# Norms of keys and queries in two chains instead of one in the mixers of a two-block transformer kernel

## The chip, the cores and the metric

The kernel runs on one core of a Trainium2 chip. The metric is the device time of one execution in microseconds (us), the median over several executions.

## The reference

Two transformer blocks of two layers each are applied to one sequence of 256 tokens with 1024 features. The change touches the second block only. Each of its two layers starts with this mixer (`DEPTH` is 2, `DN_HEADS` 4, the head size 128, `T` is 256 tokens):

```python
def l2norm(t):
    return t * lax.rsqrt(jnp.sum(t * t, -1, keepdims=True) + L2_EPS)

def gated_deltanet(q, k, v, z, b_logit, a_logit, sc_w, a_log, dt_bias, on_g):
    qkv = jax.nn.silu(causal_depthwise_conv(jnp.concatenate([q, k, v], -1), sc_w))
    q, k, v = jnp.split(qkv, 3, axis=-1)
    q, k, v = l2norm(heads(q)), l2norm(heads(k)), heads(v)
    beta = jax.nn.sigmoid(b_logit)
    g = -jnp.exp(a_log) * jax.nn.softplus(a_logit + dt_bias)
    o = chunk_gated_delta_rule(q, k, v, g, beta)
    ...

def hybrid_mixer(x, w_in, ...):
    h = x @ w_in
    c_val, c_gate, q, k, v, z, b_logit, a_logit = jnp.split(h, IN_SPLITS_2, axis=-1)
    y_conv = conformer_conv(c_val, c_gate, dw_w, dw_b, cln_g, cln_b)
    y_dn = gated_deltanet(q, k, v, z, b_logit, a_logit, sc_w, a_log, dt_bias, on_g)
    return jnp.concatenate([y_conv, y_dn], axis=-1) @ w_out
```

`conformer_conv` holds a causal depthwise convolution with a window of 31 tokens over 512 channels. `chunk_gated_delta_rule` builds 64-token triangular systems from the normed keys and queries, solves them, and runs a state through the four chunks. After the mixer come a residual, a layer norm, and a feed-forward part: a dense one in the first layer, eight experts in the second. The norms that the change is about are the two `l2norm` calls: for each head and token a sum of 128 squares, its root and its reciprocal, multiplied back onto keys and queries.

## The kernel before

Every engine has one program, written out by hand in a fixed order, and every wait is a wait on a counter of another engine (`pe_done`, `act_done`, `vec_done`, `slots_used`). So a waiting instruction holds back all that is queued behind it on its engine. `mix_tensor`, `mix_scalar` and `mix_vector` hold the mixer's three programs; they run once for `mixA` (first layer) and once for `mixB` (second layer).

TensorE multiplies the transposed activations `xT` with 12 slots of weights from a ring in SBUF that SyncE's queue fills: `project(n)` for n from 0 to 11. One such projection gives two blocks of 128 features in the bank `6 + n % 2` (n = 4 and 5 are the keys, 6 and 7 the queries, 8 and 9 the values, 10 and 11 the gate `z`). "The eighth projection" is `project(7)` and the ninth is `project(8)`. ScalarE copies each out of its bank (`evac(n)`, L1985); `project(n)` waits for `evac(n - 2)`. VectorE then runs a four-tap convolution over it (`short_conv(n)`, L2109 and L2112), and ScalarE a SiLU (`silu(n)`, L1992). For keys and queries VectorE squares the result (`square(n)`, L2120).

Between these, VectorE works off the 31-tap convolution, in portions put among the other work by hand: `taps(n)` (L2827 and L2831) is n taps of two instructions each.

The norms follow one chain for keys and queries together: sums of squares over features by matmuls with a one-hot column (L1774, four for each of k and q, into bank 5), a root on ScalarE (L2016), a reciprocal on VectorE (L2194), the high half in fp32r on ScalarE (L2019) and the low half on VectorE (L2196), and the broadcast of both halves to 128 partitions by four matmuls for each of the two (`broadcast`, L1718, steps `bck` and `bcq`). VectorE multiplies the keys with their norm (L2203), the keys with beta (L2208, from banks 0 and 1, step `bcb`), and the queries with theirs (L2212). Then come the products of keys with keys and queries (L1786), the masked matrices (L2223 to L2239), the transposes of the keys (L1743), the second half of the last projection, and the triangular solve. `row_both` holds two rows, one broadcast each; `norms` is a tile of 4 partitions with 512 columns, 256 for the keys and 256 for the queries.

The order on the engines in this stretch of the kernel before is:

- TensorE: `project(7)`, `project(8)`, the sums, `project(9)`, `bck` and `bcq`, `project(10)`, the key products.
- ScalarE: `evac(7)`, `silu(7)`, `evac(8)`, root, high half, `silu(8)`, `evac(9)`.
- VectorE: `square(7)`, `taps(8)`, reciprocal, low half, `short_conv(8)`, the three multiplications.

Of the kernel before, what the change touches and what calls it, by code (L numbers as in the profile page):

```python
# [17 lines left out]
F32 = mybir.dt.float32  # L18
# [4 lines left out]
ALU = mybir.AluOpType  # L23
AX = mybir.AxisListType

P = 128
# [114 lines left out]
def build(nc, x_d, stream, par1_d, par2_d, con_d, out, known):  # L141
    ctx = ExitStack()
    with ctx:
# [1549 lines left out]
        def mix_tensor(pe, tag, layer, last):  # L1693
# [14 lines left out]
            def project(n):  # L1708
                w = rg.take(pe).rearrange("p (k n) -> p k n", n=UNIT)
                if n >= 2:  # L1710
                    pe.wait_ge(act_done, AC.at(tag + f"ev{n - 2}"))
                project_half(n, w, 0)
                project_half(n, w, 1).then_inc(slots_used, 1)

            def broadcast(banks, j, name):

                for h in range(4):
                    mm = pe.matmul(PS[banks[h // 2]][:, (h % 2) * T:(h % 2 + 1) * T], sel_both[0:36, h * P:(h + 1) * P],  # L1718
                                   row_both[0:36, j, :], start=True, stop=True)
                mm.then_inc(pe_done, PE.step(tag + name))  # L1720
# [43 lines left out]
            pe.wait_ge(vec_done, VE.at(tag + "gb.lo"))  # L1764
            broadcast((2, 3), 0, "bcg")
            broadcast((0, 1), 1, "bcb")
            for n in range(5, 9):
                project(n)

            pe.wait_ge(vec_done, VE.at(tag + "sq"))  # L1770
            for n, name in enumerate("kq"):
                y = sq[name][:, :, :].rearrange("p t n -> p (t n)").rearrange("p (b t) -> p b t", t=T)
                for h in range(4):
                    mm = pe.matmul(PS[5][0:4, n * T:(n + 1) * T], hot[:, 3 - h:7 - h], y[:, h, :],  # L1774
                                   start=(h == 0), stop=(h == 3))
            mm.then_inc(pe_done, PE.step(tag + "ssq"))
            project(9)
            pe.wait_ge(vec_done, VE.at(tag + "kq.lo"))
            broadcast((4, 5), 0, "bck")
            broadcast((2, 3), 1, "bcq")  # L1780
            project(10)
            pe.wait_ge(vec_done, VE.at(tag + "kq"))
            for t in range(NT):
# [177 lines left out]
        def mix_scalar(act, tag, layer, last):  # L1961
# [20 lines left out]
            def evac(n):  # L1982
                act.wait_ge(slots_used, used(n + 1))
                func = {"cg": ACT.Sigmoid, "z": ACT.Silu}.get(MIX_SLOTS[n][0], ACT.Copy)
                act.activation(evac2(n), PS[6 + n % 2][:, :].rearrange("p (a b) -> p a b", a=2), func)\  # L1985
                   .then_inc(act_done, AC.step(tag + f"ev{n}"))
# [21 lines left out]
            for n in range(4, 8):  # L2008
                evac(n)
                silu(n)  # L2010
                if n == 5:
                    act.wait_ge(vec_done, VE.at(tag + "ex"))
                    act.activation(scr[:, 0, :], scr[:, 0, :], ACT.Exp).then_inc(act_done, AC.step(tag + "ET"))
            evac(8)
            act.wait_ge(pe_done, PE.at(tag + "ssq"))
            act.activation(norms, PS[5][0:4, :], ACT.Sqrt, bias=eps_rms[0:4, 0:1]).then_inc(act_done, AC.step(tag + "l2r"))  # L2016
            act.wait_ge(vec_done, VE.at(tag + "rn"))
            act.wait_ge(pe_done, PE.at(tag + "bcb"))
            act.activation(row_both[0:4, :, :], norms.rearrange("p (j t) -> p j t", j=2), ACT.Copy)\  # L2019
               .then_inc(act_done, AC.step(tag + "kq.hi"))  # L2020
            silu(8)
            evac(9)
            act.wait_ge(pe_done, PE.at(tag + "bcq"))
            act.activation(row_both[0:4, 0, :], rows[4], ACT.Copy).then_inc(act_done, AC.step(tag + "e.hi"))
            silu(9)
# [62 lines left out]
        def mix_vector(v, tag, layer, last):  # L2088
# [36 lines left out]
            def taps(n):  # L2125
                for pair, w in itertools.islice(tap, n):
                    v_taps(v, tag, pair, w, w + 1)
# [45 lines left out]
            for t in range(NT):  # L2173
                for h in range(4):
# [6 lines left out]
            short_conv(5)  # L2181
            taps(3)
            square(5)
            short_conv(6)
            taps(3)
            square(6)
# [1 line left out]
            short_conv(7)  # L2188
            taps(3)
            square(7)  # L2190
            VE.mark(tag + "sq")
            taps(8)
            v.wait_ge(act_done, AC.at(tag + "l2r"))
            v.reciprocal(norms, norms).then_inc(vec_done, VE.step(tag + "rn"))  # L2194
            v.wait_ge(act_done, AC.at(tag + "kq.hi"))
            v.tensor_tensor(row_both[32:36, :, :], norms.rearrange("p (j t) -> p j t", j=2),  # L2196
                            row_both[0:4, :, :].bitcast(F32), ALU.subtract).then_inc(vec_done, VE.step(tag + "kq.lo"))
            short_conv(8)

            v.wait_ge(pe_done, PE.at(tag + "bck"))  # L2200
            for i in range(2):
                half = slice(i * 512, (i + 1) * 512)
                v.tensor_tensor(dkf[:, half], dkf[:, half], PS[4 + i][:, :], ALU.mult).then_inc(vec_done, VE.step())  # L2203
            v_wait(v)
            v.wait_ge(pe_done, PE.at(tag + "bcb"))
            for i in range(2):
# [2 lines left out]
            v.wait_ge(pe_done, PE.at(tag + "bcq"))  # L2209
            for i in range(2):  # L2210
                half = slice(i * 512, (i + 1) * 512)
                v.scalar_tensor_tensor(out=dqf[:, half], in0=dqf[:, half], scalar=float(P) ** -0.5, in1=PS[2 + i][:, :],  # L2212
                                       op0=ALU.mult, op1=ALU.mult).then_inc(vec_done, VE.step())
            VE.mark(tag + "kq")
            short_conv(9)
# [813 lines left out]
```

## Time and profile before

| what | value |
|---|---|
| median of three runs | 2625.47 us (2623.07 to 2625.53) |
| span of the profiled execution, first to last instruction | 2620.8 us |
| median less that span | 4.7 us |
| TensorE busy | 97% of the span |
| VectorE busy | 73% |
| ScalarE busy | 53% |
| mean granted TensorE clock | 0.981 |

No time of its own is listed for the profiled execution, only its span; the three timed runs lie 2.3 to 4.8 us above it. The first mixer's stretch lies around 990 to 1184 us of the span and the second's around 1380 to 1556 us. The profile's busy times are added over the whole program; the rows below are from the stretch that the change touches. A time in a row of the chain of waits is the time that the instruction added to the chain; a time in the timeline is the instruction's duration, and overlaps its neighbour by some 0.08 us on VectorE.

### The profile page before, as it was taken

The numbers are of one execution on the slowest core, as the hardware profiler recorded it, in microseconds if no ns is written. First come the engines' busy times: TensorE is split into PE (matmuls) and PEld (weight loads), VectorE is DVE, ScalarE is ACT, GpSimd is POOL, SyncE is SP. The second block draws the span as 40 slices with busy tenths as digits, with TensorE's granted clock in tenths as the row PEclk, the third lists the DMA queues.
The fourth block names the chain that finished last, engine by engine and source line by source line (L and its number), as shares of the span: only waits on it lengthen the run. The fifth ranks groups of instructions, "written<-read, shape, count | busy, mean of one in ns | idle before, by whom it ended". The sixth has DMA issues, their size and how long they took to land.

```text
span 2620.8 us, 36271 instructions
## 1 busy us (share of the span) xinstructions
PE 2532.1 (97%) x14798; PEld 2195.6 (84%) x14798; DVE 1914.5 (73%) x2221; ACT 1399.9 (53%) x1490; POOL 0.2 (0%) x4
## 2 busy tenths in 40 slices
PE   7999999999999999999999999999999999999897
PEld 7999889899898998869988767888888888888786
DVE  7765755577675546956447958898989898988797
ACT  4554544456454433224333226777777777777674
POOL 0000000000000000000000000000000000000000
PEclk9999999999999999999999998999999999999999
DMA  6334545343345534215534117999999999999796
GB/s 252 131 128 145 201 185 193 136 155 136 114 176 199 187 150 175 97 37 221 193 145 147 49 58 270 358 362 351 355 359 358 353 352 356 354 355 361 286 355 259
DMA packets 119492, 593.19 MB, mean 226 GB/s; under 512 B 17440, under 2 KB 17824, under 8 KB 77216
## 3 DMA queue, kind: packets, MB, share of 16 engines
q1 hardware_dynamic: 110096, 585.40, 60.2%
q10 hardware_dynamic: 9232, 5.47, 0.8%
q8 instruction: 118, 1.93, 0.3%
q14 instruction: 46, 0.38, 0.0%
HBM read 589.79 MB, written 1.05 MB: 225 GB/s over the span
## 4 chain that ended last, share of the span: by engine, by line
PE 85%; DVE 12%; ACT 1%; issue 1%; DMA 1%; POOLq 0%; ACTq 0%; DVEq 0%
PE bank L2525 35%; PE bank L595 20%; PE bank L852 12%; PE bank L1704 3%; DVE big L2831 2%; PE bank L1120 2%; DVE ring_lo L826 2%; PE bank L2481 1%; PE bank L1135 1%; PE bank L1725 1%; PE bank L1890 1%; PE bank L2544 1%; DVE big L2112 1%; PE bank L1934 1%; DVE wlo L674 0%
## 5 line engine op out<-in xcount | busy, mean ns | idle before, releaser
L674 DVE TENSOR_TENSOR wlo<-ring,whi 128x2048 fp32r<-128x2048 f32 x430 | 981.4, 2290 | 167.1 <-ACT whi L669 161.7
L669 ACT ACTIVATE whi<-ring 128x2048 fp32r<-128x2048 f32 x433 | 827.9, 1914 | 132.3 <-PE bank L2525 109.7
L2525 PE MATMUL bank<-whi,xhi 128*128 128x512 f32 x896 | 362.3, 404 | 9.8 <-DVE wlo L674 7.8
L2525 PE MATMUL bank<-whi,xlo 128*128 128x512 f32 x896 | 352.3, 393 | 0.0
L2525 PE MATMUL bank<-wlo,xhi 128*128 128x512 f32 x896 | 350.7, 391 | 0.0
L826 DVE TENSOR_TENSOR ring_lo<-ring,slot_hi 128x1024 fp32r<-128x1024 f32 x160 | 192.4, 1222 | 130.1 <-ACT slot_hi L803 123.2
L595 PE MATMUL bank<-xhi,whi 128*128 128x256 f32 x864 | 245.8, 284 | 2.4 <-DVE xlo L557 1.3
L595 PE MATMUL bank<-xlo,whi 128*128 128x256 f32 x864 | 245.7, 284 | 0.0
L595 PE MATMUL bank<-xhi,wlo 128*128 128x256 f32 x864 | 245.6, 284 | 0.0
L803 ACT ACTIVATE slot_hi<-ring 128x1024 fp32r<-128x1024 f32 x160 | 166.6, 1053 | 106.8 <-PE bank L852 77.5
L852 PE MATMUL bank<-xh,slot_hi 128*128 128x256 f32 x704 | 202.4, 287 | 3.0 <-DVE ring_lo L826 3.0
L2525 PEld LDWEIGHTS bank<-whi,xhi 128*128 128x128 f32 x896 | 169.0, 189 | 42.3 <-DVE wlo L674 8.3
L2525 PEld LDWEIGHTS bank<-whi,xlo 128*128 128x128 f32 x896 | 169.1, 189 | 38.0
L852 PE MATMUL bank<-xh,ring_lo 128*128 128x256 f32 x704 | 199.8, 284 | 0.0
L852 PE MATMUL bank<-xl,slot_hi 128*128 128x256 f32 x704 | 198.1, 281 | 0.0
L2525 PEld LDWEIGHTS bank<-wlo,xhi 128*128 128x128 f32 x896 | 169.7, 189 | 32.8
L697 ACT ACTIVATE scr<-bank 128x512 f32<-128x512 f32 x43 | 25.7, 598 | 294.2 <-PE bank L595 294.2
L2525 PE MATMUL bank<-whi,hhi 128*128 128x512 f32 x448 | 177.4, 396 | 2.8 <-DVE hlo L2674 2.6
L1704 PE MATMUL bank<-xT,ring 128*128 128x256 f32 x768 | 175.0, 389 | 1.8 <-POOLq L2843 1.8
L2525 PE MATMUL bank<-whi,hlo 128*128 128x512 f32 x448 | 174.9, 390 | 0.0
L2525 PE MATMUL bank<-wlo,hhi 128*128 128x512 f32 x448 | 174.7, 390 | 0.0
L595 PEld LDWEIGHTS bank<-xhi,whi 128*128 128x128 f32 x864 | 166.9, 193 | 4.5 <-issue 3.1
(509 smaller groups left out, 4613.1 us busy)
## 6 DMA issues: line engine op xcount, KB each, us to landing
ring<-in_stream SPq DMA_DIRECT2D x555, 1024.0 KB, 6.6
par<-in_par ACTq DMA_DIRECT2D x2, 2048.0 KB, 9.3
con<-in_con SPq DMA_DIRECT2D x1, 1216.0 KB, 10.4
X<-in_x SPq DMA_DIRECT2D x2, 512.0 KB, 4.1
out_y<-X SPq DMA_DIRECT2D x2, 512.0 KB, 2.6
par<-in_par ACTq DMA_DIRECT2D x2, 448.0 KB, 5.9
par<-in_par ACTq DMA_DIRECT2D x2, 157.5 KB, 3.4
con<-in_con SPq DMA_DIRECT2D x1, 64.0 KB, 4.3
```

The source lines that it names most:

```text
L595: mm = pe.matmul(out, left, right, start=start and n == 0, stop=stop and n == len(pairs) - 1, skip_group_check=True)
L669: act.activation(whi[:, k % NSPLIT, :], src, ACT.Copy).then_inc(act_done, AC.step(tag + f".w{k}"))
L674: v.tensor_tensor(wlo[:, k % NSPLIT, :], src, whi[:, k % NSPLIT, :].bitcast(F32), ALU.subtract)\
L803: act.activation(high_half(n, half), ring[:, n % NSLOT, half * 1024:(half + 1) * 1024], ACT.Copy)\
L826: v.tensor_tensor(low_half(n, half), ring[:, n % NSLOT, half * 1024:(half + 1) * 1024], high_half(n, half).bitcast(F32), ALU.subtract)\
L852: mm = pe.matmul(bank[:, h * T:(h + 1) * T], left, right, start=first, stop=last, skip_group_check=True)
L1120: mm = pe.matmul(PS[n % 4][:, f * T:(f + 1) * T], w[:, k, cb], y[:, k, :], start=(k == 0 and i == 0), stop=(k == 3 and i == 2))
L1135: mm = pe.matmul(PS[4 + 2 * t + f][:, :], y[:, 2 * s + kk, tok], w[:, kk, halves(f)], start=(s == 0 and kk == 0 and i == 0), stop=(s == 3 ...
L1704: mm = pe.matmul(PS[6 + n % 2][:, h * T:(h + 1) * T], w[:, k, h * P:(h + 1) * P], xT[:, k, :], start=(k == 0), stop=(k == KD - 1))
L1725: mm = pe.matmul(PS[bank][:, hc], lhs[:, hc], rhs[:, hc], start=True, stop=True)
L2525: mm = pe.matmul(out, left, right, start=start and i == 0, stop=stop and i == len(pairs) - 1)
L2831: v.scalar_tensor_tensor(out=ca[:, b, :], in0=cv[:, b, w:w + T], scalar=tap, in1=ca[:, b, :], op0=ALU.mult, op1=ALU.add)\
```

## The change

Keys and queries get a chain each. On TensorE the sums of the keys' squares come behind `project(7)`, then `project(8)`, then a wait for the keys' low half, the keys' broadcast (now into banks 2 and 3), the sums of the queries' squares, `project(9)`, a wait for the queries' low half, and the queries' broadcast (now into banks 4 and 5). ScalarE takes the keys' root ahead of `evac(8)`, the keys' high half and the queries' root behind it, and the queries' high half behind `silu(8)` and `evac(9)`. VectorE runs the keys' reciprocal directly behind `square(7)`, four taps, the keys' low half, four taps, the queries' reciprocal, `short_conv(8)`, and the queries' low half. Root, reciprocal, high and low half are each done twice on 256 columns instead of once on 512.

```diff
--- before.py
+++ after.py
@@ -1764,20 +1764,25 @@
             pe.wait_ge(vec_done, VE.at(tag + "gb.lo"))
             broadcast((2, 3), 0, "bcg")
             broadcast((0, 1), 1, "bcb")
-            for n in range(5, 9):
-                project(n)
-
-            pe.wait_ge(vec_done, VE.at(tag + "sq"))
-            for n, name in enumerate("kq"):
+            def sums(n, name):
+                pe.wait_ge(vec_done, VE.at(tag + "sq" + name))
                 y = sq[name][:, :, :].rearrange("p t n -> p (t n)").rearrange("p (b t) -> p b t", t=T)
                 for h in range(4):
                     mm = pe.matmul(PS[5][0:4, n * T:(n + 1) * T], hot[:, 3 - h:7 - h], y[:, h, :],
                                    start=(h == 0), stop=(h == 3))
-            mm.then_inc(pe_done, PE.step(tag + "ssq"))
+                mm.then_inc(pe_done, PE.step(tag + "ssq" + name))
+
+            for n in range(5, 8):
+                project(n)
+            sums(0, "k")
+            project(8)
+            pe.wait_ge(vec_done, VE.at(tag + "ex"))
+            pe.wait_ge(vec_done, VE.at(tag + "k.lo"))
+            broadcast((2, 3), 0, "bck")
+            sums(1, "q")
             project(9)
-            pe.wait_ge(vec_done, VE.at(tag + "kq.lo"))
-            broadcast((4, 5), 0, "bck")
-            broadcast((2, 3), 1, "bcq")
+            pe.wait_ge(vec_done, VE.at(tag + "q.lo"))
+            broadcast((4, 5), 1, "bcq")
             project(10)
             pe.wait_ge(vec_done, VE.at(tag + "kq"))
             for t in range(NT):
@@ -2011,15 +2016,25 @@
                 if n == 5:
                     act.wait_ge(vec_done, VE.at(tag + "ex"))
                     act.activation(scr[:, 0, :], scr[:, 0, :], ACT.Exp).then_inc(act_done, AC.step(tag + "ET"))
+            def norm_row(j, name):
+                row = norms[:, j * T:(j + 1) * T]
+                act.wait_ge(pe_done, PE.at(tag + "ssq" + name))
+                act.activation(row, PS[5][0:4, j * T:(j + 1) * T], ACT.Sqrt, bias=eps_rms[0:4, 0:1])\
+                   .then_inc(act_done, AC.step(tag + "l2r" + name))
+
+            def norm_high(j, name):
+                act.wait_ge(vec_done, VE.at(tag + "rn" + name))
+                act.wait_ge(pe_done, PE.at(tag + ("bcg", "bcb")[j]))
+                act.activation(row_both[0:4, j, :], norms[:, j * T:(j + 1) * T], ACT.Copy)\
+                   .then_inc(act_done, AC.step(tag + name + ".hi"))
+
+            norm_row(0, "k")
             evac(8)
-            act.wait_ge(pe_done, PE.at(tag + "ssq"))
-            act.activation(norms, PS[5][0:4, :], ACT.Sqrt, bias=eps_rms[0:4, 0:1]).then_inc(act_done, AC.step(tag + "l2r"))
-            act.wait_ge(vec_done, VE.at(tag + "rn"))
-            act.wait_ge(pe_done, PE.at(tag + "bcb"))
-            act.activation(row_both[0:4, :, :], norms.rearrange("p (j t) -> p j t", j=2), ACT.Copy)\
-               .then_inc(act_done, AC.step(tag + "kq.hi"))
+            norm_high(0, "k")
+            norm_row(1, "q")
             silu(8)
             evac(9)
+            norm_high(1, "q")
             act.wait_ge(pe_done, PE.at(tag + "bcq"))
             act.activation(row_both[0:4, 0, :], rows[4], ACT.Copy).then_inc(act_done, AC.step(tag + "e.hi"))
             silu(9)
@@ -2181,6 +2196,7 @@
             short_conv(5)
             taps(3)
             square(5)
+            VE.mark(tag + "sqk")
             short_conv(6)
             taps(3)
             square(6)
@@ -2188,19 +2204,30 @@
             short_conv(7)
             taps(3)
             square(7)
-            VE.mark(tag + "sq")
-            taps(8)
-            v.wait_ge(act_done, AC.at(tag + "l2r"))
-            v.reciprocal(norms, norms).then_inc(vec_done, VE.step(tag + "rn"))
-            v.wait_ge(act_done, AC.at(tag + "kq.hi"))
-            v.tensor_tensor(row_both[32:36, :, :], norms.rearrange("p (j t) -> p j t", j=2),
-                            row_both[0:4, :, :].bitcast(F32), ALU.subtract).then_inc(vec_done, VE.step(tag + "kq.lo"))
+            VE.mark(tag + "sqq")
+
+            def norm_inverse(j, name):
+                row = norms[:, j * T:(j + 1) * T]
+                v.wait_ge(act_done, AC.at(tag + "l2r" + name))
+                v.reciprocal(row, row).then_inc(vec_done, VE.step(tag + "rn" + name))
+
+            def norm_low(j, name):
+                v.wait_ge(act_done, AC.at(tag + name + ".hi"))
+                v.tensor_tensor(row_both[32:36, j, :], norms[:, j * T:(j + 1) * T], row_both[0:4, j, :].bitcast(F32),
+                                ALU.subtract).then_inc(vec_done, VE.step(tag + name + ".lo"))
+
+            norm_inverse(0, "k")
+            taps(4)
+            norm_low(0, "k")
+            taps(4)
+            norm_inverse(1, "q")
             short_conv(8)
+            norm_low(1, "q")
 
             v.wait_ge(pe_done, PE.at(tag + "bck"))
             for i in range(2):
                 half = slice(i * 512, (i + 1) * 512)
-                v.tensor_tensor(dkf[:, half], dkf[:, half], PS[4 + i][:, :], ALU.mult).then_inc(vec_done, VE.step())
+                v.tensor_tensor(dkf[:, half], dkf[:, half], PS[2 + i][:, :], ALU.mult).then_inc(vec_done, VE.step())
             v_wait(v)
             v.wait_ge(pe_done, PE.at(tag + "bcb"))
             for i in range(2):
@@ -2209,7 +2236,7 @@
             v.wait_ge(pe_done, PE.at(tag + "bcq"))
             for i in range(2):
                 half = slice(i * 512, (i + 1) * 512)
-                v.scalar_tensor_tensor(out=dqf[:, half], in0=dqf[:, half], scalar=float(P) ** -0.5, in1=PS[2 + i][:, :],
+                v.scalar_tensor_tensor(out=dqf[:, half], in0=dqf[:, half], scalar=float(P) ** -0.5, in1=PS[4 + i][:, :],
                                        op0=ALU.mult, op1=ALU.mult).then_inc(vec_done, VE.step())
             VE.mark(tag + "kq")
             short_conv(9)
```

## Rows read from the trace of the kernel before

**Rows 1.** The page's first part: busy us, share of the span, instructions.

```profile
PE 2532.1 (97%) x14798; PEld 2195.6 (84%) x14798; DVE 1914.5 (73%) x2221; ACT 1399.9 (53%) x1490; POOL 0.2 (0%) x4
```

**Rows 2.** Chain that ended last, in order: start us, us, what.

```profile
1062.68 6.34 DVE big L2831 x16
1069.02 3.25 DVE smb L2194
...
1093.70 1.55 PE bank L1743 x8
1095.25 4.68 PE bank L1704 x16
1099.92 1.75 PE bank L1731 x16
...
1184.05 178.61 PE bank L595 x1272
```

**Rows 3.** Timeline of VectorE, first mixer: start us, us, what [idle before].

```profile
1068.93 3.33 DVE L2194 RECIPROCAL smb<-smb 4x512 f32<-4x512 f32 x1
1072.96 0.68 DVE L2196 TENSOR_TENSOR row_both<-smb,row_both 4x512 fp32r<-4x512 f32 x1 [0.70 <-ACT row_both L2019]
1073.67 0.62 DVE L2109 TENSOR_SCALAR big<-big,par 128x256 f32<-128x256 f32 x2
1074.20 2.46 DVE L2112 SCALAR_TENSOR_TENSOR big<-big,par 128x256 f32<-128x256 f32 x6
...
1083.30 0.41 DVE L2217 TENSOR_TENSOR row_both<-smb,row_both 4x256 fp32r<-4x256 f32 x1
1083.75 4.84 DVE L2831 SCALAR_TENSOR_TENSOR big<-big,par 128x256 f32<-128x256 f32 x12
...
1093.56 1.28 DVE L2239 TENSOR_TENSOR attn<-bank,scr 128x512 f32<-128x512 f32 x2
...
1097.91 2.49 DVE L2246 TENSOR_TENSOR big<-bank,small 128x512 f32<-128x512 f32 x4
...
1130.79 1.74 DVE L2299 RECIPROCAL big<-big 128x256 f32<-128x256 f32 x1
```

**Rows 4.** Timeline of TensorE, first mixer.

```profile
1062.74 1.89 PE L1774 MATMUL bank<-keT,hot 128*4 128x256 f32 x8 [0.20 <-DVE o_tm L2120]
...
1066.29 7.17 PE L1704 MATMUL bank<-xT,ring 128*128 128x256 f32 x32
1073.69 1.21 PE L1718 MATMUL bank<-row_both,sel_both 36*128 36x256 f32 x8 [0.23 <-DVE row_both L2196]
1074.83 7.17 PE L1704 MATMUL bank<-xT,ring 128*128 128x256 f32 x32
1081.84 3.73 PE L1786 MATMUL bank<-big 128*128 128x128 f32 x32
...
1093.70 1.55 PE L1743 MATMUL bank<-con,big 128*128 128x128 f32 x8 [3.80 <-DVE big L2236]
...
1108.65 1.04 PE L1743 MATMUL bank<-con,big 128*128 128x128 f32 x8
```

**Rows 5.** Timeline of ScalarE, first mixer.

```profile
1059.74 0.63 ACT L1992 ACTIVATE big<-big 128x512 f32<-128x512 f32 x1 [3.47 <-DVE big L2112]
1062.58 0.60 ACT L1985 ACTIVATE big<-bank 128x512 f32<-128x512 f32 x1 [2.21 <-PE bank L1704]
1063.20 1.28 ACT L2016 ACT_TABLE_LOAD   x1
1066.39 0.68 ACT L2016 ACTIVATE smb<-bank,eps_rms 4x512 f32<-4x512 f32 x1 [1.91 <-PE bank L1774]
...
1077.23 0.58 ACT L1985 ACTIVATE big<-bank 128x512 f32<-128x512 f32 x1
1077.71 0.40 ACT L2024 ACTIVATE row_both<-smb 4x256 fp32r<-4x256 f32 x1
```

**Rows 6.** Windows around the longest wait: us, busy of the engines, granted PEclk, DMA.

```profile
1091.00:1094.00 3.00, 0.30 (x3) 0.31 (x4) 2.97 (x6) 0.00 (x0) 0.00 (x0) 1.00 0.00 0
1094.00:1097.00 3.00, 3.00 (x13) 2.64 (x12) 3.00 (x8) 0.00 (x0) 0.00 (x0) 0.53 0.00 0
```

**Rows 7.** Who TensorE waited for in the second mixer: us, times, longest.

```profile
PE bank L1743 <- DVE big L2236: 3.8, 1, 3.8
```

## The prediction

> **What bounds the kernel now.** I read the page's first part first. TensorE is busy nearly all of the span, VectorE not three quarters of it [rows 1]. That is an average over stages: what the change is worth has to be read in the mixers. The second view is the chain of work that ended last, over the first mixer. From the last projections to the transposes of the keys it runs almost wholly on VectorE: the taps behind `square(7)` start at 1062.68, the reciprocal follows, and only at 1093.70 does the chain pass to TensorE's L1743 [rows 2]. The timeline of VectorE says the same: the one wait of size is 0.70 us ahead of L2196, for the high half [rows 3]. TensorE meanwhile runs ahead of VectorE and then stands still for 3.80 us ahead of L1743 [rows 4], and for 3.8 us in the second mixer too [rows 7]. So in this stretch VectorE's queue sets the time, and TensorE has some 3.8 us to spare. The dense part behind the first mixer is one long piece of TensorE, 178.61 us, in the chain [rows 2]; it begins when the mixer is done, so a shift of the mixer goes through to the end.
>
> **VectorE's own work, with no waits.** Before, from the end of `square(7)` at 1062.68 [rows 2] to the end of `short_conv(8)` at 1074.20 + 2.46 = 1076.66 [rows 3] pass 13.98 us, the wait of 0.70 in it. After, the same stretch holds two reciprocals on 256 columns, eight taps, two low halves and `short_conv(8)`. The trace has no reciprocal 4x256; the nearest row is 128x256 with 1.74 us [rows 3], against 3.33 for 512 columns, so the time goes by columns. The chain counts 3.25 for the one of 3.33 [rows 2], 0.08 less for the overlap, so I take 1.66. Bounds are 1.63 (half of 3.25) and 1.74. Eight taps are 6.34 [rows 2], four are 3.17. A low half 4x256 is 0.41 (L2217 does the same on another row), plus some 0.02 to start. `short_conv(8)` is 2.91: 3.00 from 1073.67 to 1076.66, less a start gap that I put at 0.1. Sum: 1.66 + 3.17 + 0.43 + 3.17 + 1.66 + 2.91 + 0.43 = 13.43. That is **0.55 less** than before: the wait is gone and the halving costs 0.15.
>
> **The keys' chain and the new wait on TensorE.** The keys' squares are long ready, so their sums start when `project(7)` ends. They take half of the 3.55 us from 1062.74 to 1066.29, so 1.78 [rows 4]. `project(8)` ended at about 1062.55 (its `evac` starts at 1062.58 [rows 5]); it now ends at 1062.55 + 1.78 = 1064.33. That delay itself costs nothing: `short_conv(8)` needs `evac(8)` only 8 us later. The keys' root sits behind `silu(7)`, which ends at 1060.37; with the table load of 1.28 and at most 0.68 for the root it is done by 1062.33 [rows 5], just before VectorE asks for it at 1062.68. If it came later, VectorE would wait by the difference; the margin is 0.35. VectorE's keys' low half is done at 1062.68 + 1.66 + 3.17 + 0.43 = 1067.94. TensorE has stood since 1064.33: a **new gap of 3.6 us**, in the second mixer a similar one. Behind this wait in TensorE's queue stand the keys' broadcast, the queries' sums and `project(9)`, though the last two have all that they need.
>
> **What is late next.** ScalarE's queue holds the queries' high half behind `evac(9)`, and that needs all of `project(9)`. From the keys' low half on: start 0.04, broadcast 0.57 (half of the 1.14 from 1073.69 to 1074.83), queries' sums 1.78, `project(9)` 7.17 [rows 4], start 0.02, `evac(9)` 0.48 (1077.23 to 1077.71), high half 0.40 [rows 5], start 0.02: **10.48 us**. In that time VectorE has four taps, a reciprocal and `short_conv(8)`: 3.17 + 1.66 + 2.91 = 7.74. Then its low half waits 10.48 - 7.74 = **2.74 us**. The queries' root and `silu(8)` lie within these 10.48 us on ScalarE and are ready: the root needs the sums 2.4 us after the keys' low half and VectorE asks at 3.2. Everything behind the queries' low half on VectorE waits too: even the keys' multiplication, whose broadcast is there 8 us earlier. So the earlier keys win nothing.
>
> **The clock.** During the 3.80 us ahead of L1743 TensorE does nearly nothing, and in the next three microseconds its granted clock is 0.53, mostly the lower of the two levels, 1.2 instead of 2.4 GHz [rows 6]. The work there shows the price: L1743 takes 1.55 us against 1.04 later [rows 4], and the half projection behind it 4.68 us against 3.59, half of 7.17 [rows 2, 4]: 1.6 us together. The new gap is nearly as long, and what follows it is the very path of 10.48 us. Bounds: nothing, if the clock stays up or is low only within the gap, and 1.6 us with the whole price. I take 1.5, since the gap is like that one and continuous work follows.
>
> The Trainium skill ("TensorE: Matmul & The Clock Gate", section "Why this matters for your kernels") speaks against the change here: it advises against long gaps between bursts of matmuls, because TensorE falls back to half rate. By that rule both mixers pay the 1.5; with the clock left up the sum below would be 3.0 us smaller. The trace agrees for the gap of 3.80 us (0.53).
>
> **What comes back.** TensorE's work from the queries' broadcast to the key transposes is, at full clock, 0.57 + 7.17 + 3.73 + 0.57 + 3.59 = 15.6 us [rows 4]. VectorE's, from the queries' low half to L2239, is 1093.56 - 1076.66 = 16.9 us as before [rows 3]. So TensorE's wait ahead of L1743 shrinks from 3.80 to about 1.3 us, and the low clock behind it should go. That makes TensorE 1.6 us earlier relative to VectorE at 1099.92, but the fourth of the transposes L1731 needs L2246, done at 1097.91 + 2.49 = 1100.40 [rows 3]. Before, this transpose began after three quarters of 1.75 us, at 1101.23 [rows 2]; it can move up by 0.8. I take **0.7**; bounds 0 and 0.8.
>
> **The other edits** have one answer. Banks 2 and 3 for the keys need the decay's exponents read out, which VectorE did ahead of `short_conv(5)`. Two activations more on ScalarE, about 0.8 us, lie in its idle time (it waits 2.21 and 1.91 us in the same stretch [rows 5]). The order root, copy, copy, root, SiLU needs the same two table loads. Weight slots of `project(8)` and `project(9)` are freed 2 to 6 us later; no transfer stands in the chain there [rows 2].
>
> **Sum.** Per mixer -0.55 + 2.74 + 1.5 - 0.7 = +3.0 us. Twice is +6.0. Against the profiled execution the span becomes 2620.8 + 6.0 = 2626.8; the median of the runs lies 4.7 above that span, so I forecast 2625.5 + 6.0 = **2631.5 us**.
>
> **The rivals.** (a) The forecast: wait and low clock, +4.5 to +7.5. Chance 0.55. (b) Not slower: the wait comes, but the clock stays up behind the new gap, because some of the gap's neighbours count as work. Place: `bck` to `project(9)`. Price: 2 x (-0.55 + 2.74 - 0.7) = +3.0 us, 2628.5, which is within 0.2%. It decides from about 0.75 us per mixer saved on the clock. For it: the gap is 0.2 us shorter than the one that lost the clock. Against: that one lost it [rows 6], and four thin broadcasts of 36 rows follow. Chance 0.26. (c) The shift is absorbed behind the mixer, or the 2.74 is less because ScalarE gets the high half out sooner: near 0, 2625.5. Against: `evac(9)` is ahead in an in-order queue, and the chain runs through the mixer on both sides. Chance 0.06. (d) Faster: VectorE never waits, and TensorE keeps its clock: 2 x (-0.55 - 0.8) = -2.7 us, still within 0.2%; faster by more needs something unseen. Chance 0.05, of which 0.03 beyond 0.2%. (e) Worse: the clock stays low longer, or also falls ahead of L1743, so that nothing comes back: 2 x (3.0 + 0.7 + 0.8) = +9.0, 2634.5. Chance 0.08.
>
> **How the numbers follow.** 0.2% is 5.3 us, about what a measurement of this kernel can tell from no change. The forecast lies just above it. Of (a) I put 0.48 above and 0.07 below, and all of (e) above: slower 0.56. Same is 0.07 + 0.26 + 0.06 + 0.02 = 0.41, faster 0.03. The range from 2627.0 to 2634.0 holds (a), (b) less 1.5 us of scatter (the three runs spread over 2.5), and most of the way to (e); it leaves out (c), (d) and the end of (e).
>
> **What would show it.** VectorE: an idle of 2.7 to 4.4 us ahead of the queries' low half, released by ScalarE, in both mixers; none ahead of either reciprocal over 1 us. TensorE: about 3.6 to 4.2 us ahead of `bck`, then a clock near 0.5; some 1.3 us ahead of L1743 with full clock behind. If the reciprocal of 256 columns costs much more than 1.74 us, the keys' one adds the excess to the path, and the queries' one takes it off the wait. Wrong at the root would be: no wait ahead of the queries' low half, or the wait there while the mixer's end has not moved.

## The result and the profile after

The changed kernel took 2629.09 us in the median of twelve executions (2623.52 to 2633.94), the kernel before 2623.77 in twelve beside it. The ratio is 1.0019, 95% interval 1.0011 to 1.0026: some 5 us slower, close to the 0.2% that the prediction named as the border. The forecast was +6.0 us and 2631.5, its range 2627.0 to 2634.0. The sum is nearly right, but the working is not: one term was too small by half, and a stretch that the prediction left out gives part of the loss back. So it is partly luck that the number came out so near.

The profiled execution took 2631.60 us with a span of 2629.6, so only 2.0 us lie around the span, not the 4.7 that I had taken from the median.

The timeline of VectorE after, first mixer:

```profile
1064.06 1.73 DVE L2212 RECIPROCAL smb<-smb 4x256 f32<-4x256 f32 x1
1065.73 3.14 DVE L2858 SCALAR_TENSOR_TENSOR big<-big,par 128x256 f32<-128x256 f32 x8
1068.90 0.41 DVE L2216 TENSOR_TENSOR row_both<-smb,row_both 4x256 fp32r<-4x256 f32 x1
1069.34 3.25 DVE L2858 SCALAR_TENSOR_TENSOR big<-big,par 128x256 f32<-128x256 f32 x8
1074.69 1.74 DVE L2212 RECIPROCAL smb<-smb 4x256 f32<-4x256 f32 x1 [2.09 <-ACT smb L2022]
1076.36 0.51 DVE L2124 TENSOR_SCALAR big<-big,par 128x256 f32<-128x256 f32 x2
1076.79 2.45 DVE L2127 SCALAR_TENSOR_TENSOR big<-big,par 128x256 f32<-128x256 f32 x6
1083.05 0.41 DVE L2216 TENSOR_TENSOR row_both<-smb,row_both 4x256 fp32r<-4x256 f32 x1 [3.81 <-ACT row_both L2028]
```

The reciprocal of half the columns takes 1.73 us against 3.33 [rows 3], as taken. Where VectorE waited 0.70 us before [rows 3], it now waits 2.09 and 3.81: first for the queries' root, then for their high half. The first wait was not forecast ("none ahead of either reciprocal over 1 us").

The timeline of TensorE after, same stretch:

```profile
1069.46 1.19 PE L1718 MATMUL bank<-row_both,sel_both 36*128 36x256 f32 x4 [4.20 <-DVE row_both L2216]
1070.58 3.57 PE L1771 MATMUL bank<-o_tm,hot 128*4 128x256 f32 x8
1074.08 8.01 PE L1704 MATMUL bank<-xT,ring 128*128 128x256 f32 x32
1083.52 0.74 PE L1718 MATMUL bank<-row_both,sel_both 36*128 36x256 f32 x4 [1.43 <-DVE row_both L2216]
1084.19 7.17 PE L1704 MATMUL bank<-xT,ring 128*128 128x256 f32 x32
...
1100.62 1.09 PE L1743 MATMUL bank<-con,big 128*128 128x128 f32 x8 [1.38 <-DVE big L2263]
1101.55 3.62 PE L1704 MATMUL bank<-xT,ring 128*128 128x256 f32 x16
```

And the windows of the same stretch (us, busy of PE, PEld, DVE, ACT, POOL, granted PEclk, DMA):

```profile
1065.00:1069.00 4.00, 0.26 (x2) 0.00 (x0) 3.97 (x10) 0.95 (x2) 0.00 (x0) 1.00 0.63 233
1069.00:1072.00 3.00, 2.54 (x8) 1.40 (x9) 2.97 (x8) 0.00 (x0) 0.00 (x0) 0.50 0.09 38
1072.00:1075.00 3.00, 3.00 (x8) 1.21 (x6) 0.91 (x3) 0.79 (x2) 0.00 (x0) 0.50 0.00 0
```

The new gap is 4.20 us. Behind it the clock is at its lower level, 1.2 GHz, for the six microseconds from 1069 to 1075, which hold the keys' broadcast and the queries' sums. Four matmuls of a broadcast busy the engine for 1.19 us instead of 0.74, the eight of the sums for 3.57 instead of 1.89 [rows 4], the projection for 8.01 instead of 7.17. Ahead of L1743 the wait fell from 3.80 [rows 4] to 1.38, and L1743 and the half projection take 1.09 and 3.62 us: that clock is back, as forecast. In the second mixer a fall comes on top of this: behind the wait of 1.43 us ahead of the queries' broadcast `project(10)` takes 8.86 us instead of 7.17.

```profile
1474.05 8.86 PE L1704 MATMUL bank<-xT,ring 128*128 128x256 f32 x32
```

The second mixer shows the same waits:

```profile
DVE row_both L2216 <- ACT row_both L2028: 3.1, 1, 3.1
DVE smb L2212 <- ACT smb L2022: 2.1, 1, 2.1
DVE big L2250 <- PE bank L1791: 0.5, 1, 0.5
```

To compare kernels whose mixers start at different times I cut each mixer in stretches by VectorE's instructions. A goes from the end of `square(7)` to the start of L2223, the first use of the key products. B goes from the first copy behind the squared matrices (L2259 before) to the negated `w` (L2303 before). C, the chunk stage, goes from there to the gated output (L2356 before). Times in us, first and second mixer, one profiled execution each; under C in brackets the time for which the clock was low in it:

| kernel | A | B | C |
|---|---|---|---|
| before | 25.8, 25.8 | 29.8, 29.8 | 30.9 (6.8), 30.9 (6.8) |
| after | 31.3, 30.6 | 29.2, 29.2 | 27.8 (0), 32.1 (10.2) |

A is 5.1 us longer in the mean, B 0.6 shorter. C was not in the prediction at all, and it moves by up to 4.4 us within one kernel; it is as long as the time at the low clock makes it, from 27.8 us with none to 32.1 with 10.2.

### The profile page after: what moved, and what is told of

Same layout as the page of the kernel before. It is cut to its first block, busy times and chain, and to the rows that moved or that the text cites. A ratio compares the mean times of both kernels' runs of the same rounds, so it can differ in the third digit from the quotient of the medians.

```text
span 2629.6 us, 36283 instructions
## 1 busy us (share of the span) xinstructions
PE 2536.4 (96%) x14798; PEld 2195.1 (83%) x14798; DVE 1914.6 (73%) x2225; ACT 1401.5 (53%) x1494; POOL 0.2 (0%) x4
## 4 chain that ended last, share of the span: by engine, by line
PE 85%; DVE 12%; ACT 1%; issue 1%; DMA 1%; POOLq 0%; ACTq 0%; DVEq 0%
PE bank L2552 35%; PE bank L595 20%; PE bank L852 12%; DVE big L2858 3%; PE bank L1704 2%; DVE ring_lo L826 2%; PE bank L1120 2%; PE bank L2508 1%; PE bank L1135 1%; PE bank L1725 1%; PE bank L1895 1%; PE bank L2571 1%; DVE big L2127 1%; PE bank L1939 1%; PE bank L986 0%
## 6 DMA issues: line engine op xcount, KB each, us to landing
con<-in_con SPq DMA_DIRECT2D x1, 1216.0 KB, 10.2
```

## The experiments

All ran beside the kernel before on the same chip, with its median at 2624.92 us for the first four, 2624.39 for the next four and 2624.34 for the last four. Ratios are to that kernel. The letters A, B and C in "theory A" and the like are those of the expectations; A, B and C alone are the stretches above.

**Work in the gap, too much of it (fill_gap).**

```diff
             pe.wait_ge(vec_done, VE.at(tag + "ex"))
+            for k in range(16):
+                pe.matmul(PS[2][:, 0:T], xT[:, k % KD, 0:P], xT[:, k % KD, :], start=True, stop=True)
             pe.wait_ge(vec_done, VE.at(tag + "k.lo"))
```

> The changed kernel, with sixteen matmuls without use (128x256 outputs, the time of half a projection's double pass, about 3.5 us) between the ninth projection and the wait for the keys' low half, so that TensorE works through the gap. They change nothing that is computed. Theory A (queue wait and low clock both cost): the clock no longer falls behind the gap, VectorE's wait ahead of the queries' low half is 2.7 us and none ahead of the queries' reciprocal; per mixer -0.55 + 2.74 - 0.7 = +1.5, so +3.0 us against the kernel before, and the scatter of the executions shrinks to that of the kernel before. Theory B (the clock is the whole loss): about -2.5 us against before. Theory C (the clock costs nothing): as the changed kernel, +5 us.

2630.48 us, ratio 1.0022 (1.0012 to 1.0032). I had counted one record of the trace for each matmul; it has two for each, 7.07 us in all, and they hold the keys' broadcast up by 2.8 us. A took 30.9 us in both mixers: the clock stayed high behind the gap, but the time went into the useless work. It tells nothing apart; fill_half, below, is sized by it.

**High half of the queries at once (high_first).**

```diff
             norm_row(1, "q")
+            norm_high(1, "q")
             silu(8)
             evac(9)
-            norm_high(1, "q")
```

> The changed kernel, but ScalarE makes the queries' high half directly behind the queries' root, ahead of the SiLU and the evacuation of the tenth projection. Theory A: VectorE no longer waits ahead of the queries' low half; TensorE's gap of 3.6 to 4.2 us and the low clock stay, so the queries' root still comes up to 2 us late, and the queries' broadcast stands behind a slow project(9): VectorE waits 0.5 to 2.5 us there in place of 2.7 to 3.8. Against before +1 to +4 us for both mixers. Theory B (the clock alone): as the changed kernel, +5 us, with the wait only moved.

2631.31 us, ratio 1.0024 (1.0015 to 1.0034), slower than theory A's range; by the time alone theory B, +5 us, would fit better. The stretch did what theory A has: A took 27.9 us in both mixers, 3.1 less than in the changed kernel, with one wait of 2.1 us left for the queries' root and one of 0.3 for their broadcast. C took 30.5 in both with 6.8 us of low clock, and that is where the gain went in this profile. But its execution took 2626.67 us, 4.6 under the median, and nine of the other ten were slower than it, all nine with a lower mean clock (0.977 to 0.979 against 0.980). Where their time went no profile shows.

**Sums of the queries ahead of the wait (sums_first).**

Besides, the sums and the root of the queries move to bank 4 (not shown).

```diff
             project(8)
+            sums(1, "q")
             pe.wait_ge(vec_done, VE.at(tag + "ex"))
             pe.wait_ge(vec_done, VE.at(tag + "k.lo"))
             broadcast((2, 3), 0, "bck")
-            sums(1, "q")
```

> The changed kernel, but the sums of the queries' squares come directly behind the ninth projection, ahead of the wait for the keys' low half (into bank 4 in place of bank 5). Theory A: the gap on TensorE shrinks from 3.6 to 1.8 us, the clock stays high behind it, and the path from the keys' low half to the queries' high half loses 1.78 us: VectorE waits 1.0 us. Per mixer -0.55 + 1.0 - 0.7 = -0.3: -0.6 us against before, no difference. Theory C (the clock costs nothing and the wait is all): +5 - 3.6 = +1.5 us.

2623.63 us, ratio 0.9998 (0.9989 to 1.0007): no difference, as theory A had it; the interval does not rule out theory C's +1.5 us. A took 26.8 and 28.2 us against 26.3 by the expectation. In the second mixer the clock fell behind a gap of 2.4 us, which speaks against theory C: `project(9)` took 8.86 us, and VectorE waited 2.9 us for the high half, where it waited 1.5 in the first.

**Both moves (both_orders).** The two diffs above together.

> The changed kernel with both moves: the sums of the queries' squares ahead of the wait for the keys' low half, and the queries' high half directly behind their root on ScalarE. Theory A: no wait of size on VectorE between square(7) and L2250, no low clock in the gap nor ahead of the key transposes: per mixer -0.55 - 0.7 = -1.25, -2.5 us against before, 0.1% faster. If the halving or the moves cost something that I do not see, it comes out at the time of before or above.

2617.34 us, ratio 0.9975 (0.9964 to 0.9985), three times the gain expected. A is 25.3 us in both, 0.5 less than before, without a wait of VectorE; B is 29.2. That makes the 2.1 us of the expectation. The other 5 us are not in A or B. Of these, C has 2.0, with 32.1 and 27.8; for the rest the profile is a poor witness, since its execution took 2619.67 and five of the eight took 2617.2 to 2617.3.

**Work in the gap, the right size (fill_half).** As fill_gap, with `range(8)`.

> As fill_gap, but with eight matmuls without use in place of sixteen: one such matmul takes 0.44 us at full clock by fill_gap's trace (sixteen took 7.07 us, more than the gap, so they held up the keys' broadcast by 2.8 us). Eight take 3.5 us and fit into the gap of 3.6 to 4.2. Theory A (the queue wait and the low clock both cost): the clock stays high from the keys' broadcast to the evacuation of the tenth projection, no wait ahead of the queries' reciprocal, 2.7 us ahead of the queries' low half, +3.0 us against before and executions that scatter less than the changed kernel's. Theory B (the clock is the whole loss): -2.5 us. Theory C (the clock costs nothing): +5 us.

2622.15 us, ratio 0.9993 (0.9984 to 1.0002), 4.3 under the changed kernel measured beside it. The windows of its first mixer:

```profile
1068.00:1072.00 4.00, 4.00 (x21) 3.08 (x20) 3.94 (x11) 0.56 (x2) 0.00 (x0) 1.00 0.75 262
1072.00:1076.00 4.00, 4.00 (x20) 2.66 (x18) 4.00 (x9) 1.75 (x2) 0.00 (x0) 1.00 0.02 4
```

and VectorE's timeline:

```profile
1074.13 1.74 DVE L2214 RECIPROCAL smb<-smb 4x256 f32<-4x256 f32 x1
...
1081.63 0.41 DVE L2218 TENSOR_TENSOR row_both<-smb,row_both 4x256 fp32r<-4x256 f32 x1 [2.96 <-ACT row_both L2030]
```

The clock is 1.00 in these 8 us, the wait for the queries' root is gone, and the wait for their high half is 2.96 us. A took 28.3 and 28.2 us. So the queue's wait alone makes A 2.4 us longer than before (forecast 2.2), and the low clock adds 2.3 to 3.0 more in the changed kernel (forecast 1.5). (It falls only later in the first mixer: behind the gap of 1.43 us `project(10)` took 8.86 us, without making A longer.) The median is below theory A's +3.0 by 5 us, though, and would fit theory B's -2.5; the wait of 2.96 us and A are what speak against B. C took 27.8 in both mixers, 6.4 less than before.

**The changed kernel again (after_again).** No edit.

> The changed kernel once more, for a second profile and more executions: its times fell into two groups, 2623.5 to 2626.6 us at a mean clock of 0.984 and 2631.6 to 2633.9 at 0.978 to 0.980, and the profile showed one of the second. If the two groups are the low clock in the mixers, a profile of the first group has less time at the low clock between square(7) and L2250, and VectorE's waits there are near 2.7 us; one of the second group has them at 5 to 6 us again. If the groups have another cause, the waits are the same in both.

2626.49 us, ratio 1.0017 (1.0007 to 1.0028). Seven of ten executions took 2624.4 to 2627.3, three 2633.4 to 2634.8. The profile was one of the lower group, at 2625.61 us. A took 30.9 and 31.1 us: no shorter than in the execution of 2631.60. C took 27.8 in both. So my expectation fell: the groups are not made by the low clock in A, which both have. Of the 6.0 us between the two spans, 4.4 are in C of the second mixer. The windows that hold C in the second mixer, first of the execution at 2631.60:

```profile
1527.00:1552.00 25.00, 22.90 (x130) 18.73 (x130) 12.37 (x22) 4.31 (x9) 0.00 (x0) 0.80 0.00 1
```

then of the one at 2625.61:

```profile
1530.00:1550.00 20.00, 17.89 (x106) 12.47 (x105) 10.74 (x22) 5.15 (x9) 0.00 (x0) 1.00 0.01 2
```

A second place that no edit touches differs as well, the start of the dense part behind the first mixer. The same two executions, in the same order:

```profile
1185.00:1192.00 7.00, 6.33 (x30) 5.96 (x30) 5.84 (x14) 4.20 (x9) 0.00 (x0) 0.51 0.99 412
1185.00:1192.00 7.00, 4.91 (x40) 4.66 (x41) 5.94 (x14) 3.62 (x7) 0.00 (x0) 1.00 1.00 418
```

From the first mixer's gated output to the second's `square(7)` the first took 288.2 us and the second 286.8.

**The old gap filled (before_fill).** Eight such matmuls into bank 6 in the kernel before, where it lost its clock.

```diff
+            pe.wait_ge(act_done, AC.at(tag + "ev10"))
+            for k in range(8):
+                pe.matmul(PS[6][:, 0:T], xT[:, k % KD, 0:P], xT[:, k % KD, :], start=True, stop=True)
             pe.wait_ge(vec_done, VE.at(tag + "qg"))
             turn_tokens((4, 5), dk, "trk")
```

> The kernel before, with eight matmuls without use (3.5 us at full clock, into bank 6) ahead of the transposes of the keys, where TensorE stood for 3.8 us and lost its clock. Theory A (what the prediction took as given back): the clock stays high behind it, L1743 and the half projection take 1.6 us less, and 0.7 us of it reaches the end in each mixer: -1.4 us. Rival: nothing comes through, because VectorE's L2246 is the later one: 0. If the low clock matters more than I think downstream, it is below -2.5 us.

2619.49 us, ratio 0.9978 (0.9969 to 0.9987). L1743 takes 1.10 us and B 29.2 in both mixers, 0.6 less each: that is the term called 0.7. The median is 4.9 us under the kernel before, where theory A had 1.4; B accounts for 1.1 of them. Four executions took 2613.0 to 2615.3, eight 2619.3 to 2622.0. The profile is one of the eight, and its C had 29.3 and 30.9.

**The halving alone (halves_only).** Root, reciprocal, high and low half in two halves, in the order of the kernel before. TensorE's and VectorE's part of the edit (the queries' sums in bank 4 and ScalarE's order, both roots behind `evac(8)` and then both high halves, are not shown):

```diff
             for n in range(5, 8):
                 project(n)
+            project(8)
             sums(0, "k")
-            project(8)
-            pe.wait_ge(vec_done, VE.at(tag + "ex"))
-            pe.wait_ge(vec_done, VE.at(tag + "k.lo"))
-            broadcast((2, 3), 0, "bck")
             sums(1, "q")
             project(9)
+            pe.wait_ge(vec_done, VE.at(tag + "ex"))
             pe.wait_ge(vec_done, VE.at(tag + "q.lo"))
+            broadcast((2, 3), 0, "bck")
             broadcast((4, 5), 1, "bcq")
...
+            taps(8)
             norm_inverse(0, "k")
-            taps(4)
+            norm_inverse(1, "q")
             norm_low(0, "k")
-            taps(4)
-            norm_inverse(1, "q")
+            norm_low(1, "q")
             short_conv(8)
-            norm_low(1, "q")
```

> The changed kernel's halved root, reciprocal, high and low half, but in the order of the kernel before: both sums behind the ninth projection (keys' into bank 5, queries' into bank 4), both broadcasts behind the tenth, keys' and queries' steps directly behind one another. Theory A: the halving itself costs VectorE 0.07 us for the reciprocals and 0.15 for the low halves; the wait for the high half overlaps with the second reciprocal: per mixer -0.5 to +0.3 us, within 0.5 us of before for both. If the halving cost more than that, it would be a cause beside the order: +1 us or more.

2621.37 us, ratio 0.9986 (0.9977 to 0.9995). A took 25.4 us in both mixers, 0.4 less than before: the second reciprocal covers the wait for the first high half. The halving is no cause of the loss. The median is 3 us under the kernel before, more than the 0.5 expected; 0.9 of them come from A and 0.6 from B of the second mixer.

**Both causes taken away, in the other way (high_fill).** fill_half and high_first together.

> The changed kernel with eight matmuls without use in the gap (as fill_half) and the queries' high half directly behind their root (as high_first). From square(7) to the key products' first use the kernel before takes 25.8 us, the changed one 30.6 to 31.3, fill_half 28.2, high_first 27.9, both_orders 25.3. Theory A (two causes that add: 2.7 us for the queue wait on ScalarE, about 2.9 for the low clock behind the gap): 25.3 us here, as in both_orders, and a median 4 to 8 us under before. Theory D (one cause, each edit takes away the same loss): about 28 us, and the median of fill_half.

2618.04 us, ratio 0.9979 (0.9970 to 0.9988), 6.3 us under the kernel before. A took 25.3 us in both. The two causes add: from 31.0 us the order on ScalarE takes 3.1 alone, the filled gap 2.8 alone, both 5.7.

**A shorter gap without useless work (low_at_once).**

```diff
             norm_inverse(0, "k")
-            taps(4)
             norm_low(0, "k")
-            taps(4)
+            taps(8)
```

> The changed kernel, but VectorE makes the keys' low half directly behind their reciprocal, and all eight taps after it. TensorE's gap ahead of the keys' broadcast shrinks from 3.6 or 4.2 to about 1.4 us without any useless work. Theory A: VectorE waits some 0.9 us for the keys' high half (behind the evacuation of the ninth projection), the clock stays high, and the path to the queries' high half has 10.9 us of VectorE's work beside it, so no wait there: 26.2 us from square(7) to the first use of the key products. If the clock falls behind 1.4 us too: 27 to 28 us.

2622.58 us, ratio 0.9992 (0.9983 to 1.0002). A took 28.0 and 27.3 us, the second of the two cases. TensorE's timeline in the first mixer:

```profile
1066.02 0.70 PE L1718 MATMUL bank<-row_both,sel_both 36*128 36x256 f32 x4 [1.52 <-DVE row_both L2216]
1066.65 3.33 PE L1771 MATMUL bank<-o_tm,hot 128*4 128x256 f32 x8
```

and its windows:

```profile
1067.00:1070.00 3.00, 3.00 (x9) 0.74 (x6) 3.00 (x9) 0.00 (x0) 0.00 (x0) 0.50 0.53 224
1070.00:1074.00 4.00, 4.00 (x18) 3.56 (x19) 4.00 (x8) 1.75 (x2) 0.00 (x0) 0.96 0.02 4
```

Here a gap of 1.52 us, and 0.70 us of broadcast behind it, were followed by the low clock, 0.50, and the sums took 3.33 us. In the second mixer it was the same behind a gap of 1.60 us.

**Work in the chunk stage (chunk_fill).** The changed kernel with eight small matmuls there.

```diff
+            def idle_work(n):
+                for k in range(n):
+                    pe.matmul(PS[4][:, 0:P], xT[:, k, 0:P], xT[:, k, 0:P], start=True, stop=True)
+
+            idle_work(2)
             pe.wait_ge(vec_done, VE.at(tag + "nw"))
             state(0)
+            idle_work(3)
             minus_w(1)
+            idle_work(3)
             state(1)
```

> The changed kernel, with eight small matmuls without use (128x128, 0.22 us each) between the first steps of the chunk stage, where TensorE waits 0.5 to 0.8 us three times. In the profiles so far the clock fell there for 0, 3.4, 6.8 or 10.2 us, and the stretch from the negated w to the gated output took 27.8, 29.3, 30.9 or 32.1 us, whichever kernel it was. Theory E (this makes the two groups of the changed kernel's times, 2624 to 2627 and 2631 to 2635): the clock stays high there, the stretch takes 27.8 to 28.5 us in both mixers, and all executions fall into the lower group, at 2623 to 2628. If the groups have another cause, both remain.

2624.36 us, ratio 1.0001 (0.9993 to 1.0010). All eleven executions lie between 2623.4 and 2626.8, as theory E had it: the upper group is gone. (The changed kernel itself did not run beside this one; nine of its 22 executions were in the upper group.) A is still 31.0 and 31.1 us. The windows that hold C:

```profile
1141.00:1161.00 20.00, 19.91 (x131) 15.08 (x130) 11.12 (x23) 4.85 (x8) 0.00 (x0) 1.00 0.01 2
1530.00:1550.00 20.00, 19.91 (x130) 15.08 (x129) 11.13 (x23) 4.85 (x8) 0.00 (x0) 1.00 0.00 1
```

In the kernel before, the 20 us around the same place were busy for 17.9 and had a clock of 0.83 in each mixer:

```profile
1133.00:1153.00 20.00, 17.90 (x98) 13.92 (x98) 9.55 (x20) 4.25 (x7) 0.00 (x0) 0.83 0.00 1
1522.00:1542.00 20.00, 17.90 (x100) 14.15 (x99) 9.81 (x20) 4.25 (x7) 0.00 (x0) 0.83 0.00 0
```

**Both moves and the work in the chunk stage (both_chunk).**

> both_orders with the same eight small matmuls in the chunk stage. The profile of both_orders had 32.1 us in the first mixer's chunk stretch and 27.8 in the second's. Theory E: 27.8 to 28.5 in both, and 2613 to 2616 us in place of 2617.2. If the small matmuls only lengthen the stage: 2618 to 2620.

2615.45 us, ratio 0.9970 (0.9958 to 0.9982), all six executions between 2614.1 and 2616.3, as theory E had it. A is 25.3, B 29.2 and C 27.8 us in both mixers. This is the fastest by its median, 8.9 us under the kernel before; the two moves alone, without useless matmuls, give 7.6 of them.

The stretches of all kernels, first and second mixer:

| kernel | median, us | A | B | C |
|---|---|---|---|---|
| after_again | 2626.49 | 30.9, 31.1 | 29.2, 29.2 | 27.8, 27.8 |
| fill_gap | 2630.48 | 30.9, 30.9 | 29.2, 29.2 | 32.1, 32.1 |
| fill_half | 2622.15 | 28.3, 28.2 | 29.2, 29.2 | 27.8, 27.8 |
| high_first | 2631.31 | 27.9, 27.9 | 29.2, 29.2 | 30.5, 30.5 |
| sums_first | 2623.63 | 26.8, 28.2 | 29.2, 29.2 | 30.9, 29.3 |
| both_orders | 2617.34 | 25.3, 25.3 | 29.2, 29.2 | 32.1, 27.8 |
| high_fill | 2618.04 | 25.3, 25.3 | 29.2, 29.2 | 29.3, 27.8 |
| before_fill | 2619.49 | 25.8, 25.8 | 29.2, 29.2 | 29.3, 30.9 |
| halves_only | 2621.37 | 25.4, 25.4 | 29.8, 29.2 | 27.8, 30.5 |
| low_at_once | 2622.58 | 28.0, 27.3 | 29.2, 29.2 | 32.1, 27.8 |
| chunk_fill | 2624.36 | 31.0, 31.1 | 29.2, 29.2 | 27.8, 27.8 |
| both_chunk | 2615.45 | 25.3, 25.3 | 29.2, 29.2 | 27.8, 27.8 |

A and B go with the kernel; C is a matter of the single execution. Between A and B all have 14.2 to 14.8 us, the longer ones where VectorE waited up to 0.6 us for the key products, in six of the eleven because `project(10)` ran at the low clock. What lies outside all these stretches, some 2420 us, varies from 2417.0 to 2421.4 us over the fourteen profiles.

## Why the prediction was right, and where it was not

- **VectorE's own work, -0.55 us.** Right. both_orders has no wait and shows -0.5; the reciprocal on half the columns took 1.73 us against the 1.74 of the row that I went by.
- **The queue's wait, +2.74.** Right, shown by fill_half: 2.96 us with the clock high. It goes away when the high half no longer stands behind `evac(9)` (high_fill).
- **The clock, +1.5.** Right in kind and too small; this is the term mis-sized most. I had carried over the price of the fall behind the old gap, 1.6 us, as the upper bound. The changed kernel against fill_half shows 2.3 to 3.0 us in each mixer. In the first, TensorE's busy times grow by 0.45 for the broadcast, 1.68 for the sums and 0.84 for the projection: 3.0 us. The low clock lasted 6.8 us here, against 3.4 behind the old gap, and fell on the path that VectorE waits for. The rule of the Trainium skill ("TensorE: Matmul & The Clock Gate", "Why this matters for your kernels") against long gaps holds for the gap of 4.20 us; the runs show the fall behind shorter ones too (last section).
- **"None ahead of either reciprocal over 1 us."** Wrong, by the same term. The slow sums bring the queries' root late, and VectorE waits 2.09 us for it. The prediction let the sums be done 0.8 us before VectorE asks and left out the root itself, 0.47 us in the trace of the changed kernel; so even its own 1.5 us of low clock, which falls on the broadcast and the sums first, would have made the root late. It costs nothing on top, since the wait for the high half follows on the same path; high_first shows that it is what is left when the other is gone.
- **What comes back, -0.7.** Right: -0.6 in B, and before_fill shows the same 0.6.
- **The sum.** From A and B the change costs 4.2 to 4.9 us in each mixer, about 9 us for both, where I had 6.0. It measured 5. So two errors cancel: the low clock's term was too small, and some 4 us come back that the sum did not have. By the profiles most of it comes back in the chunk stage, which the prediction left out as unchanged. C took 30.9 us twice before, and 27.8 in three of the four stretches after. With the clock held up there (chunk_fill) the changed kernel's upper group is gone. That the kernel before meets the low clock there more often than the others is what the medians suggest: all but high_first's lie 1.5 to 9.3 us lower against it than A and B account for. Each execution's mean clock points the same way: 0.979 to 0.983 in the 91 of the kernel before beside the experiments (one more, of 5234.53 us, left aside), 0.983 to 0.985 in the changed kernel's lower group and 0.978 to 0.980 in its upper one. But it is a mean over the whole program and does not say where. It is not shown, because there are only one or two profiles of each, and high_first, 3.4 us higher than A and B say, does not fit. The kernel before with the small matmuls of chunk_fill would decide it; it was not run. Why it should be so stays open.
- **The base.** The span's surroundings are 2.0 us and not 4.7: the profiled execution of the kernel before was itself among the shorter ones. As the forecast was made as a difference, this did not enter it.

Rival (b), the clock staying high, is out: it fell behind the new gap in both mixers of both profiles. Rival (c) is out too: the mixers did get longer. Rival (d), no wait at all, is not what the change did; it is what both_orders did, with -2.1 us in A and B against its -2.7. Of rival (e), a clock low for longer, the first half came true, 6.8 us; with the full clock ahead of L1743 coming back all the same. Its +9.0 is about what A and B together cost.

## What to carry to other kernels

Splitting a chain in two moves the first half's wait into a queue: ask what stands behind it there, and on which other queue the second half's next step stands behind the work so delayed. Here two lines in the wrong place, the queries' sums behind a wait and their high half behind an evacuation, made a change of about -1 us into one of +4.5 in each mixer, by A and B; with them moved, the same split beats both kernels, the one before by 0.25%. A clock fall is not to be priced by the nearest one in the trace, only bounded by the length of work that is exposed behind it. And before a difference of 0.2% is explained by one stretch, look at how much the others vary from one execution to the next.

## What the hardware showed that was not expected

- The granted clock fell to 0.50 behind a gap of 1.52 us in low_at_once, with TensorE busy for more than 10 us ahead of it, and in the changed kernel's second mixer one of 1.43 us was followed by a `project(10)` of 8.86 us instead of 7.17. Gaps as long did not lose it elsewhere: in the first mixer the same gap of 1.43 us was followed by one of 7.17, and in both_orders a gap of 1.61 us by a `project(9)` of 7.17. So the length of a gap alone does not tell whether the clock falls.
- Dense stretches with short waits can lose the clock too: the chunk stage, busy for 17.9 of 20 us, was granted 1.00 in some executions and 0.83 in others. With eight small useless matmuls in waits of 0.5 to 0.8 us it was 1.00 in both mixers, and the spread of the changed kernel's times was 3.4 us instead of 10.4.
- Useless matmuls can pay: the kernel before was 4.9 us faster with 3.6 us of them in each old gap, of which stretch B accounts for 1.1.
